# Squares of x added on GpSimd, and their column sums moved into the third dense unit, at the seam to the first layer

## The reference, cut to what matters

```python
h_lat = h_lat + gate_l[:, None] * merge(ssd_l, gdn_l, z_l, h_lat.dtype)   # merge ends in rms_norm(y @ w_out, post_w)

def _rmsnorm(x, g):
    x32 = x.astype(jnp.float32)
    y = x32 * lax.rsqrt(jnp.mean(x32 * x32, axis=-1, keepdims=True) + EPS)
    return (y * g.astype(jnp.float32)).astype(x.dtype)
```

## Time and profile before

| | |
|---|---|
| median of 3 runs | 3031.02 us (3030.68 to 3032.49) |
| the profiled execution's own time | 3031.7 us |
| its span, first to last instruction | 3029.9 us |
| PE busy | 2989.5 us (99%) |
| DVE busy | 1853.7 us (61%) |
| ACT busy | 1335.1 us (44%) |
| GpSimd busy | 192.7 us (6%) |
| mean granted TensorE clock | 0.994 of full speed |
| the seam, in this execution | about 855 us to 887 us |

### The profile page before, as it was taken

One profiled execution on the slowest core, in us unless ns is written; L12 is line 12 of the kernel. 1 busy time (PEld: TensorE's weight loads), 2 busy tenths in 40 slices (PEclk: granted clock), 3 DMA queues, 4 the chain that ended last, 5 costly groups with the idle time before them and its releaser, 6 DMA issues.

```text
span 3029.9 us, 68077 instructions
## 1 busy us (share of the span) xinstructions
PE 2989.5 (99%) x28670; PEld 2823.5 (93%) x28670; DVE 1853.7 (61%) x2510; ACT 1335.1 (44%) x1731; POOL 192.7 (6%) x287
## 2 busy tenths in 40 slices
PE   6999999999999999999999999999999999999999
PEld 2688888888999999999999999999999999999999
DVE  3677777688876666555455555566665555555554
ACT  3455455445454444444343333444444443333333
POOL 0000000000100001110010000100012110000000
PEclk8999999999999999999999999999999999999999
DMA  9612211323955444555555555554545555555554
GB/s 398 274 58 85 85 66 76 125 87 113 397 199 203 172 179 172 189 194 194 192 192 192 192 191 194 220 180 168 178 170 187 192 192 193 193 194 193 194 194 152
DMA packets 82964, 547.13 MB, mean 181 GB/s; under 512 B 9125, under 2 KB 13365, under 8 KB 18928
## 3 DMA queue, kind: packets, MB, share of 16 engines
q1 hardware_dynamic: 78448, 523.27, 47.6%
q10 hardware_dynamic: 2192, 15.40, 1.3%
q0 software_dynamic: 2160, 6.05, 0.6%
HBM read 540.46 MB, written 7.36 MB: 181 GB/s over the span
## 4 chain that ended last, share of the span: by engine, by line
PE 95%; DMA 2%; DVE 1%; PEld 0%; ACT 0%; issue 0%; PEldq 0%; ACTq 0%; DVEq 0%
PE bank L443 29%; PE bank L444 28%; PE bank L445 28%; DMA raw<-stream 2%; PE bank L845 1%; PE bank L718 1%; PE bank L712 1%; PE bank L948 1%; PE bank L754 1%; PE bank L1147 0%; PE bank L931 0%; PE bank L770 0%; PE bank L956 0%; PE bank L1155 0%; DMA pars<-pars 0%; PE bank L771 0%
## 5 line engine op out<-in xcount | busy, mean ns | idle before, releaser
L422 ACT CAST w_hi<-raw 128x2048 fp32r<-128x2048 f32 x443 | 847.9, 1914 | 1225.0 <-PE bank L445 1225.0
L427 DVE TENSOR_TENSOR w_lo<-raw,w_hi 128x2048 fp32r<-128x2048 f32 x443 | 1017.8, 2298 | 550.1 <-ACT w_hi L422 550.0
L443 PE MATMUL bank<-a_lo,w_hi 128*128 128x256 f32 (+1 forms) x3568 | 1060.7, 297 | 1.1 <-DVE w_lo L427 0.5
L444 PE MATMUL bank<-a_hi,w_lo 128*128 128x256 f32 (+1 forms) x3568 | 1035.1, 290 | 0.0
L445 PE MATMUL bank<-a_hi,w_hi 128*128 128x256 f32 (+1 forms) x3568 | 1035.0, 290 | 0.0
L443 PE MATMUL bank<-h_lo,w_hi 128*128 128x256 f32 x3552 | 990.5, 279 | 3.8 <-DVE h_lo L2108 3.8
L444 PE MATMUL bank<-h_hi,w_lo 128*128 128x256 f32 x3552 | 981.7, 276 | 0.0
L445 PE MATMUL bank<-h_hi,w_hi 128*128 128x256 f32 x3552 | 981.5, 276 | 0.0
L443 PEld LDWEIGHTS bank<-a_lo,w_hi 128*128 128x128 f32 x3568 | 672.5, 188 | 25.5 <-DVE g_X L1881 2.7
L445 PEld LDWEIGHTS bank<-a_hi,w_hi 128*128 128x128 f32 x3568 | 670.4, 188 | 17.3
L444 PEld LDWEIGHTS bank<-a_hi,w_lo 128*128 128x128 f32 x3568 | 671.7, 188 | 12.4
(11 more groups left out here) (353 smaller groups left out, 2127.9 us busy)
## 6 DMA issues: line engine op xcount, KB each, us to landing
raw<-stream SPq DMA_DIRECT2D x485, 1024.0 KB, 4.8
gate_raw<-stream ACTq DMA_DIRECT2D x12, 1024.0 KB, 8.3
xr<-x_t SPq DMA_DIRECT2D x4, 1024.0 KB, 16.3
q_raw<-stream SPq DMA_DIRECT2D x8, 512.0 KB, 9.6
x_res<-x_t SPq DMA_DIRECT2D x1, 2048.0 KB, 16.6
bias_table<-bias SPq DMA_DIRECT2D x1, 2048.0 KB, 10.8
bias<-bias_table ACTq DMA_DIRECT2D x1, 2048.0 KB, 10.7
out_t<-x_res SPq DMA_DIRECT2D x4, 512.0 KB, 5.3
```

What stands on the lines that cost most here:

```text
L422: act.copy(w_hi[u.slot][:], raw[u.raw][:]).then_inc(hi_ready, 1)
L427: dve.tensor_tensor(w_lo[u.slot][:], raw[u.raw][:], w_hi[u.slot][:], ALU.subtract).then_inc(lo_ready, 1)
L443: pe.matmul(acc, wh, lo[:, k, 0:n], start=(k == first), stop=False)
L444: pe.matmul(acc, wl, hi[:, k, 0:n], start=False, stop=False)
```

## The change

The squares of x are no longer summed tile by tile on PE. ACT still makes all sixteen, now alternately in `n_sq` and `b_gc`. GpSimd clears `n_acc` and adds the first fifteen squares into it, one by one; each addition raises `x_sq_used`, on which ACT's reuse of the buffer waits, and GpSimd waits for it too. PE makes only two sums over ones, of the total and of the last square, and it makes them inside the third unit, between its sixth and its seventh tile. The first half of the third unit's weights is rounded on ACT before the last four squares instead of between them.

```diff
@@ gpsimd, between the issue at line 674 and the one at line 676
+            def square_added(i, j):
+
+                pool.wait_ge(S["x_sq"], i * 2 + (j + 1))
+                return pool.tensor_tensor(n_acc[:], n_acc[:], (n_sq, b_gc)[j][:], ALU.add)
+
+            pool.wait_ge(S["ss_mm"], 1)
+            own.link(pool.memset(n_acc[:], 0.0))
+            with pool.Fori(0, KT // 2 - 1) as i:
+                for j in range(2):
+                    square_added(i, j).then_inc(S["x_sq_used"], 1)
+                    pool.wait_ge(S["x_sq_used"], i * 2 + (j + 1))
+            square_added(KT // 2 - 1, 0).then_inc(S["acc_ready"], 1)
@@ tensor, norm_sums
-                pe.wait_ge(S["acc_ready"], e + 1 - (e > 1))
+                pe.wait_ge(S["acc_ready"], e + 1)
                 mm(psum[2][:, 0:L], ONES, n_acc[:], start=True, stop=False)
-                if e == 0:
-                    pe.wait_ge(S["mo_sq"], KT)
-                mm(psum[2][:, 0:L], ONES, n_sq[:] if e else hbuf[:, 3 * L:4 * L], start=False, stop=True
+                if e < 2:
+                    pe.wait_ge(S["x_sq" if e else "mo_sq"], KT)
+                mm(psum[2][:, 0:L], ONES, {0: hbuf[:, 3 * L:4 * L], 1: b_gc[:]}.get(e, n_sq[:]), start=False, stop=True
                    ).then_inc(S["ss_mm"], 1)
@@ tensor, first_normed
                 for k in range(KT):
                     unit_mm(pe, u, h_hi3, h_lo3, L, ready, part=(k, k + 1))
                     unit_mm(pe, second, h_hi3, h_lo3, L, part=(k, k + 1))
-                    for s in (*((k - 3, k - 2) if k % 2 and k > 2 else ()), *((k - 1, k) if k == KT - 1 else ())):
-                        pe.wait_ge(S["x_sq"], s + 1)
-                        mm(psum[2][:, 0:L], ONES, (n_sq, n_acc)[s % 2][:], start=(s == 0), stop=(s == KT - 1)
-                           ).then_inc(S["x_sq_used" if s < KT - 1 else "ss_mm"], 1)
@@ tensor, head
-                        unit_mm(pe, u.ahead(2), h_hi3, h_lo3, L, (lo_ready, {8: u.ahead(2).split}), split=False)
+                        ready = (lo_ready, {8: u.ahead(2).split})
+                        unit_mm(pe, u.ahead(2), h_hi3, h_lo3, L, ready, part=(0, 6), split=False)
+                        norm_sums(1)
+                        unit_mm(pe, u.ahead(2), h_hi3, h_lo3, L, ready, part=(6, KT), split=False)
@@ scalar
                         weighted_hi(0, 0, k)
+                        if k == KT - 1:
+                            split_act_half(Unit(U_LAYER + 2), 0)
                         for s in (*((k - 3, k - 2) if k % 2 and k > 2 else ()), *((k - 1, k) if k == KT - 1 else ())):
                             if s >= 2:
                                 act.wait_ge(S["x_sq_used"], s - 1)
-                            f((n_sq, n_acc)[s % 2][:], x_res[:, s * L:(s + 1) * L], ACT.Square).then_inc(S["x_sq"], 1)
-                            if s == KT - 3:
-                                split_act_half(Unit(U_LAYER + 2), 0)
+                            f((n_sq, b_gc)[s % 2][:], x_res[:, s * L:(s + 1) * L], ACT.Square).then_inc(S["x_sq"], 1)
                     split_act_half(Unit(U_LAYER + 2), 1)
```

## The result

| | kernel before | changed kernel |
|---|---|---|
| median of 20 runs each | 3031.94 us (3030.68 to 3036.3) | 3037.4 us (3035.51 to 3039.15) |
| ratio | | 1.0018 (95%: 1.0012 to 1.0024) |
| span of the profiled execution | 3029.9 us | 3036.0 us |
| PE busy | 2989.5 us (99%) | 2984.3 us (98%) |

The change costs 5.5 us (0.0012 to 0.0024 of 3032 us is 3.6 to 7.3). The ratio lies under the bound of 0.2% that the prediction took for no change, though its interval reaches over it, and 20 runs of each tell the loss apart from nothing. 3037.4 lies exactly on the upper edge of the range (3029.0 to 3037.4) and 3.0 over the 3034.4 forecast; 0.9 of that is the kernel before itself, whose median was 3031.02 over the first three runs and is 3031.94 over 20.

The account below looks back on a forecast made before the run. PE was taken to bound the seam's later part (2.29 us for two tiles), DVE close behind (2.25). Shift 12 d - 1.7, with d 0.45, gave +3.7, taken as +3.4: 3034.4 us, range 3029.0 to 3037.4.

Parts of the forecast that it names:

- A: Likeliest case: GpSimd's additions hold DVE off in the seam, 0.3 to 0.55 us each; 3033 to 3036 us; chance 0.57.
- Step 1: DVE undisturbed takes 1.124 us a tile in the seam, so x would be complete on PE's side at 874.8.
- Step 2: Twelve GpSimd additions beside DVE's unbroken work cost it 0.45 us each, 5.4 us; tile 15 ready at 880.2.
- d: DVE's delay from one GpSimd addition: taken as 0.45 us, bounds 0 and 0.74; shift 12 d - 1.7.
- Step 3: Third unit's weights: rounding on ACT, then DVE's 1.23 us subtraction; the unit starts at 881.9, against 879.90 before.
- Step 4: Inside the third unit: no wait or a few tenths for the total, second weight half costs nothing; end at 888.5.
- Step 5: After the root, the fourth unit's weights are rounded and subtracted; it starts at 890.3, not 886.6: 3.7 us later.
- What costs nothing: Clearing `n_acc`, ACT's waits on `x_sq_used`, and the later table transfer, landing at 901 at worst, before SP's copy at 903.92.
- B: Additions slip into gaps between DVE's seam instructions, d near 0: shift -1.7, 3029.3 us; chance 0.22.
- C: PE's clock falls again, third unit starts at 1.2 GHz: 2.4 us more, 3036.8 us; chance 0.10.
- D: Each addition keeps DVE off for its whole 0.74 us in the seam: +7.2, 3038.2 us; chance 0.07.
- E: DVE's chain in the seam does not bind and PE gets its sums back: -6.0 us, 3025.0; chance 0.02.

Follow-up runs that it names:

- write-only run: Changed kernel with each of GpSimd's fifteen additions replaced by a clearing write of the same tile, loop written out: 3031.55 against 3031.33 us, ratio 0.9999.
- the series: Changed kernel with GpSimd's additions as memset, 256-column copy, 128-column addition, or left at 256 columns: ratios 0.9999, 0.9999, 1.0005, 1.0018.
- the four seams of before: Kernel before, unaltered, first trace and three repeats, first `h_lo` to fourth unit's second matmul: 28.47, 28.62, 27.22, 27.32 us.

## Why the prediction was right, and by how much it was off

Its direction, the mechanism of its likeliest case (A) and its outer range held; the loss was 5.5 us timed where I had taken 3.4, and A's own range, 3033 to 3036, was missed by 1.4 us. Part of that was luck. The time lies on the very edge of the range, and passes the 3037.08 from which I had counted it as slower; that the ratio stays under 0.2% owes to the kernel before, whose median came out 0.9 us above the one I had used. Starts of after are 859.61 - 858.24 = 1.37 later than those of before for reasons ahead of the seam, and are told here less that.

**Step 1, DVE without disturbance: right.** The write-only run has DVE at 2.26 us for two tiles and a shift of -1.6 against the same trace for a fixed part of -1.7. Its `h_lo` of tile 15 ends 16.5 us after the first begins, and the working had 874.8 - 858.24 = 16.6.

**Step 2, the additions: right in mechanism, under in size.** d is 0.49 us, where I took 0.45 out of 0 to 0.74. Twelve times 0.04 is 0.48 us. I had gone under the row's 0.47 since DVE's fixed part would hide some; the series does show a fixed part that DVE is not held for, 0.25 us of an addition's 0.74, but the row's 0.47 was already net of it. The Trainium skill's page SBUF — State Buffer, section "Who interferes with whom", has such a pair contend for a port that it calls an exclusive lock, and excepts a GpSimd instruction that only writes. The traces agree with both, in the stretched instructions and in the memset that costs nothing. A block for the whole of the first they do not show: the additions of 862.87 and 863.83 had 0.67 and 0.69 us left when DVE's next instruction began, and it grew by 0.47 and 0.49.

**Step 3, the third unit: right.** 883.75 - 1.37 = 882.4 for 881.9, all of it from d: the last `h_lo` ends at 882.02, and 0.45 for ACT and 1.23 for the subtraction follow, as summed.

**Step 4, inside the third unit: right, with the few tenths it allowed.** Six tiles end at 883.75 + 2.12 = 885.87, the last addition at 885.40 + 0.74 = 886.14, and the first sum starts at 886.20: 0.3 us of waiting for the total, most of the 0.4 that the series leaves over for the full addition. The second half's low part is ready at 886.60 + 1.23 = 887.83, and PE comes to it at 887.88: it costs nothing, as worked out, but only just.

**Step 5, root and fourth unit: right.** 892.78 - 1.37 = 891.4 for the second matmul, 4.7 later than 886.71. The working gave 3.7, from a first matmul that I had put at 886.6 from the second; its row has 886.19. By second matmuls, the mark that counts, the working gives 3.8 (890.3 + 0.22 - 886.71), and the rest is 0.5 from d, 0.3 from step 4 and 0.1 of handoffs.

**The sum.** I took +3.4 for a worked +3.7, arguing that step 3 might be shorter. No row bore that, and it was wrong: 0.3. The measured +4.7 is against a trace with the long low clock. Against the mean of the four seams of before it is 33.2 - 27.9 = 5.3, which is the 5.5 of the times. This last 0.6 us is the one thing whose kind I had not seen: the kernel before has a PE-bound seam that varied by 1.2 us or more with the clock, and I took one draw of it for its value. In all, the 2.1 us between 3.4 and 5.5 are 0.3 taken off without a row, 0.1 of the mark, 0.5 of d, 0.3 of the wait for the total, 0.1 of handoffs, 0.6 of the draw, and 0.2 between seams and times.

**What costs nothing: right.** The table's issue is at 886.09 and landed 5.0 us later, well ahead of SP's copy:

```profile
910.00 0.43 SPq L603 DMA_DIRECT2D bias_table<-bias  x1
```

**Rivals.** B (additions in DVE's gaps) fell by 862.99 to 866.23 in the changed kernel; the write-only run is what it would have looked like. C (the clock falls) fell by the 1.00 from 865 to 893, the third unit included. D (0.74 for each) fell by d = 0.49. E (PE gets its sums back) fell by the write-only run, whose seam is 0.3 to 1.7 us shorter than those of before and not 6.0. Where the 6.0 us went: DVE needs 2.25 us for two tiles, and from its first `h_lo` to the end of the last 16.5 us undisturbed, where the kernel before took 16.9 to 18.3. So up to the third unit no more than 0.4 to 1.8 us could come back, and the reading additions then push DVE to 3.22 us for two tiles.

What stays open: whether the two lengths of the low clock have a cause in the program or outside it. No run here varied what PE does ahead of its standstill.

## What to carry to other kernels

Before work is taken off the busiest engine, look at the engine next behind it at that place: here DVE stood at 2.25 us against PE's 2.29, and the work moved without contention gave 0.3 to 1.7 of 6.0 us. An idle GpSimd is not free help for a stretch in which DVE works without a break on two tensors of SBUF; here each of its instructions that read there cost DVE all but a quarter of a microsecond of its length, so look for such a pair of instructions anywhere in the trace and multiply by their number. One trace of before is one draw: where PE is the bound and its clock is low for part of the stretch, take several. If the work can be made cheaper where it is (0.12 in place of 0.43 us for a sum), that comes first.

## What the runs showed of the hardware

- A GpSimd addition of 128x256 float32 holds DVE's two-tensor instruction off by 0.49 us, one of 128x128 by 0.21, a copy of 128x256 by 0.14 and a memset not at all; GpSimd itself loses at most 0.08 us then. At the later norm it was GpSimd that waited 1.9 us for one long instruction of DVE. In each place read here, the instruction that was stretched by more than 0.1 us was the one that had begun second.
- The clock stayed at 1.00 while PE was busy for 8.79 of 15 us (865 to 880 in the changed kernel).
- After the same standstill of PE the low clock lasted longer in some executions than in others, worth 1.2 to 1.4 us to a stretch that PE bounds (27.2 and 27.3 against 28.5 and 28.6) and nothing (33.17 and 33.20) to one that DVE bounds.
